# Order of the pieces in the second slab of a woven pair of column tiles

## The reference

```python
u = rms_norm(h, norm_pre_mix[l])
p = (u @ w_in[l]).astype(jnp.float32)
p_ret, p_hgrn, p_ml, p_rw = split_cols(p, GROUP_COLS)
o_ret = retention_group(p_ret)
o_hgrn = hgrn2_group(p_hgrn, lower_bounds[l], hgrn_norm_w[l])
o_ml = mlstm_group(p_ml, ...)
o_rw, v_first = rwkv7_group(p_rw, v_first, ...)
mixed = jnp.concatenate([o_ret, o_hgrn, o_ml, o_rw], axis=-1).astype(h.dtype) @ w_out[l]
```

## Time and profile before

| what | value |
|---|---|
| median of 3 runs | 3970.29 us (3957.03 to 3972.97) |
| profiled execution, its own time | 3960.19 us |
| its span, first to last instruction | 3958.4 us |
| mean granted clock of TensorE | 0.965 of full |
| TensorE busy | 3662.7 us, 93% |
| VectorE, ScalarE, GpSimd busy | 2039.9, 1771.8, 1729.3 us |
| woven matmuls (lines 604 to 606) | 7776 of 25724 |

### The profile page before, as it was taken

One profiled execution on the slowest core, in us unless ns is written; L12 is line 12 of the kernel. 1 busy time (PEld: TensorE's weight loads), 2 busy tenths in 40 slices (PEclk: granted clock), 3 DMA queues, 4 the chain that ended last, 5 costly groups with the idle time before them and its releaser, 6 DMA issues. The chain is left out here.

```text
span 3958.4 us, 60887 instructions
## 1 busy us (share of the span) xinstructions
PE 3662.7 (93%) x25724; PEld 3249.1 (82%) x25724; DVE 2039.9 (52%) x2013; ACT 1771.8 (45%) x1860; POOL 1729.3 (44%) x824
## 2 busy tenths in 40 slices
PE   8898899899999999898999899999998989889988
PEld 7788888788888887787888688888887788888877
DVE  4747533655555555647532655555555443344454
ACT  4415444544443444416444544443445345444434
POOL 0426565599991000425666499993000155530000
PEclk9999899999999999998999999999999999999999
DMA  5423345477775554423345477775554533335543
GB/s 190 138 66 123 117 144 187 160 239 240 240 239 176 185 186 130 146 67 110 122 128 181 157 244 245 238 238 179 183 190 165 167 121 118 111 128 179 170 152 125
DMA packets 378828, 655.47 MB, mean 166 GB/s; under 512 B 13713, under 2 KB 189921, under 8 KB 377745
## 3 DMA queue, kind: packets, MB, share of 16 engines
q1 hardware_dynamic: 363248, 596.98, 46.3%
q0 software_dynamic: 15392, 55.79, 4.2%
HBM read 645.37 MB, written 6.29 MB: 165 GB/s over the span
## 5 line engine op out<-in xcount | busy, mean ns | idle before, releaser
L214 PE MATMUL ps<-x_parts,w_hi 128*128 128x512 f32 x6160 | 2191.0, 400 | 89.8 <-DVE x_parts L1294 25.4
L215 PE MATMUL ps<-x_parts,w_lo 128*128 128x256 f32 x6160 | 1734.7, 282 | 0.0
L193 DVE TENSOR_TENSOR w_lo<-weight_ring,w_hi 128x2048 fp32r<-128x2048 f32 x392 | 950.1, 2424 | 1057.0 <-ACT w_hi L185 1056.8
L214 PEld LDWEIGHTS ps<-x_parts,w_hi 128*128 128x128 f32 x6160 | 1169.3, 190 | 382.3 <-issue 60.9
L185 ACT ACTIVATE w_hi<-weight_ring 128x2048 fp32r<-128x2048 f32 (+1 forms) x412 | 787.8, 1912 | 1168.3 <-PE ps L215 1108.4
L215 PEld LDWEIGHTS ps<-x_parts,w_lo 128*128 128x128 f32 x6160 | 1174.9, 191 | 0.0
L604 PE MATMUL ps<-x_parts,w_hi 128*128 128x256 f32 x2592 | 781.3, 301 | 68.3 <-ACT arena L622 34.2
L605 PE MATMUL ps<-x_parts,w_hi 128*128 128x256 f32 x2592 | 746.8, 288 | 0.0
L606 PE MATMUL ps<-x_parts,w_lo 128*128 128x256 f32 x2592 | 745.5, 288 | 0.0
L604 PEld LDWEIGHTS ps<-x_parts,w_hi 128*128 128x128 f32 x2592 | 510.7, 197 | 100.6 <-issue 57.6
L555 POOL TENSOR_TENSOR w_lo<-weight_ring,w_hi 128x1024 fp32r<-128x1024 f32 (+1 forms) x152 | 377.8, 2485 | 340.7 <-ACT w_hi L552 333.5
(11 more groups left out here) (403 smaller groups left out, 2840.7 us busy)
## 6 DMA issues: line engine op xcount, KB each, us to landing
weight_ring<-in_w_in SPq DMA_DIRECT2D x212, 1024.0 KB, 5.2
weight_ring<-in_w_ffn_gate SPq DMA_DIRECT2D x88, 1024.0 KB, 5.2
weight_ring<-in_w_ffn_up SPq DMA_DIRECT2D x88, 1024.0 KB, 5.2
weight_ring<-in_w_ffn_down SPq DMA_DIRECT2D x88, 1024.0 KB, 5.2
spare<-in_w_ada POOLq DMA_DIRECT2D x96, 512.0 KB, 4.4
weight_ring<-in_w_out SPq DMA_DIRECT2D x32, 768.0 KB, 4.6
weight_ring<-in_w_out SPq DMA_DIRECT2D x24, 1024.0 KB, 5.1
weight_ring<-in_w_br_a SPq DMA_DIRECT2D x8, 1024.0 KB, 5.1
```

The source lines that it names most:

```text
L193: (ops or core.nc.vector).tensor_tensor(core.w_lo[:, g % 2, at], core.ring[:, (self.start + g) % RING, at], core.w_hi[:, g % 2, at].bitcas ...
L214: mm(out, hi, core.x_parts[:, x, :, :].rearrange("p a t -> p (a t)"), start=first, stop=False)
L215: return mm(out[:, 0:T], lo, core.x_hi[:, x, :], start=False, stop=last)
```

## The change

The list of pieces is built slab by slab. An even slab keeps its order. In an odd slab the first column tile takes the upper and the lower part, then the second tile does: (0, upper), (0, lower), (1, upper), (1, lower). The splits that are owed at the end of a list become a list for each engine in place of a single entry. Nothing else is touched; the conditions (`ends_upper`, `ends_slab`, the waits in `pe`, the reads in `act`) are as before and now meet the pieces in the new order.

```diff
--- before.py
+++ after.py
@@ -481,7 +481,12 @@
         self.ks = k // P // 2
         super().__init__(core, 2 * len(pairs), 0)
         self.slot = self.ks * self.PAIR
-        self.pieces = [(g, c, part) for g in range(self.n_slabs) for part in range(2) for c in range(self.tiles(g))]
+        self.pieces = []
+        for g in range(self.n_slabs):
+            if g % 2 == 0:
+                self.pieces += [(g, c, part) for part in range(2) for c in range(self.tiles(g))]
+            else:
+                self.pieces += [(g, c, part) for c in range(self.tiles(g)) for part in range(2)]
 
     def tiles(self, g):
         return len(self.pairs[g // 2][1])
@@ -496,7 +501,7 @@
         self.begin(after)
         self.after = after
         self.issued = dict(pe=0, act=0, sp=0, pool=0)
-        self.owed = dict(act=None, sp=None, pool=None)
+        self.owed = dict(act=[], sp=[], pool=[])
         self.begun = {"act": False, "sp": False, "pool": False}
         self.goal, self.planned, self.first_split = [], 0, self.split
 
@@ -572,14 +577,13 @@
         left = self.goal[step] - 1 - n
         late = step == len(self.goal) - 1 and left <= (0 if name == "act" else 1) and g + 2 < self.n_slabs
         if late:
-            assert self.owed[name] is None
-            self.owed[name] = (g + 2, part)
+            self.owed[name].append((g + 2, part))
         return late
 
     def paid(self, name):
 
-        g, self.owed[name] = self.owed[name], None
-        return [] if g is None else [g]
+        due, self.owed[name] = self.owed[name], []
+        return due
 
     def pe(self, pe, step):
```

## The result

The changed kernel takes 3986.45 us (median of 20 runs, 3972.02 to 3998.18), the kernel before 3970.39 (20 runs, 3957.03 to 3980.02). The ratio is 1.0044 with an interval of [1.0034, 1.0053]: 16 us slower, within 0.5% but outside my range of 3948 to 3979, and on the other side than the 1.5 us that I had won.

What follows compares the result with a forecast made beforehand. TensorE, busy 93% of the span, was taken as the bound, its weave waits being ScalarE's bank reads (50.1 us at most). Terms 2.8 + 0.6 + 0.2 - 0.8 - 1.3 = 1.5 us won gave 3968.8 us, range 3948 to 3979.

Steps and rivals of the forecast that it cites:

- f: GpSimd's upper splits start one piece later, lower parts are wanted one earlier; margins of 5.14 us become 3.70 and 2.74, no wait.
- a: Four waits in the HGRN stage: the read of bank 0 starts 0.95 us earlier; 2.8 us won (1.9 to 3.8).
- one-tile pair: In HGRN: loses its margin of 0.59 us and comes 0.4 us late, but hidden by GpSimd's split for the next stream.
- d: End of the RWKV output stage, twice: the bank read now follows the last piece; 0.8 us lost, nothing if hidden.
- rival for slower: GpSimd's later upper splits starve TensorE, 0.63 us for each meeting, 24 us in all, 3994 us; chance 3%.
- e: Norms ending retention (0.45 us later, twice) and HGRN (about 0.2, twice), upper split in the read's place; 1.3 us lost.
- b: Two waits in the MLSTM stage: a wait for bank 1 replaces that for bank 0; 0.6 us won (-0.8 to 1.8).
- c: One wait of 3.31 us in attention B: read 0 moves into the rope stage; net 0.2 us won (-0.4 to 0.9).
- bank waits as a whole: Rival for faster: TensorE's waits for bank reads vanish altogether, 50.1 us, giving 3920 us; chance 2%.
- clock's 6 us: Halved clock after idle times: shifts re-deal its length, up to 1.26 us each, about 6 us with random signs; chance 8%.

Runs made afterwards that it cites:

- e7: Kernel before, with the new order only in slabs 1 and 3 beside HGRN, 1 beside mLSTM, 1 and 3 beside attention B: 3970.87 us against 3970.41, ratio 1.0009.
- e9: Changed kernel with the old order in slabs 1 and 3 beside HGRN: 3983.65 us against 3968.29 for the kernel before, ratio 1.0034.
- e3: Changed kernel with the old order in slabs 7, 9 and 11 beside RWKV: 3975.63 us, ratio 1.0024 to the kernel before.
- e1: Changed kernel with the old order in slab 9 beside mLSTM: 3981.73 us against 3967.09 for the kernel before, ratio 1.0030.
- e8: Changed kernel whose VectorE maximum at mLSTM reads one operand from PSUM instead of its SBUF copy, leaving out the absolute value: 3969.72 us, one run.

## Why the prediction was wrong

**What bounds the kernel** was right: bank reads, not splits, are what TensorE waits for in the weave. It was also the blind spot. I took TensorE's waits as the list of all that the change could touch.

**f was the step that failed.** It asked only whether a later subtraction leaves TensorE without weights, found margins of 2.74 us and more, and gave GpSimd's shift a price of zero. That half was right for the steady stretches and wrong in the HGRN loop, where it had put the margins at over 7 us: a wait of 0.5 to 0.6 us for line 572 in each layer (see **a**). The one-tile pair, put at "hidden", shows a wait of 0.24 us. The other half was not asked: which VectorE instructions the moved subtraction now lies beside, and who waits for those. What the runs showed in its place is that the moved subtraction holds VectorE. It measured 1.28 + 1.98 us in the solve stage, 0.5 + 1.1 of the output stretch's 0.92 + 1.48 (d's 0.4 each taken off; the two waits for line 2439 grew by 1.7 together), and 1.3 + 1.3 at the end of mLSTM: 7.5 us. I had the rule and a row for it (5.77 us) and applied them to GpSimd alone, because in that row GpSimd is the one held. In the kernel before, VectorE rows of 2.46 us stood beside lines 555 and 567 in the same loop, 24 us earlier. The rival for slower had the right pair of engines with, for the most part, the wrong victim.

**a, HGRN's four waits.** At the start the step was right: 2.50 became 1.65, 10.14 became 9.19, 6.18 became 5.62. A wait of 0.41 for bank 1 is new behind the first, where I had 0.14 us to spare, and the second of the first layer, 6.21, became 7.07. Behind the second wait TensorE is 1.09 us further on in both layers (349.12 - 314.46 against 352.91 - 319.34, and 1845.06 - 1803.19 against 1858.46 - 1817.68, each from the start of the stage). But none of it is left at the end of the stage, +0.85 and +0.19 us with e's part in it. Most of it is lost in the first head of the loop, from piece 20 to piece 28 of the 68 of this weave. That stretch before and after (columns as in the section above), and TensorE's wait in it, after:

```profile
357.20:374.94 17.74, 17.74 (x175) 1.00 0.44 139
361.19:379.69 18.50, 17.99 (x175) 1.00 0.55 172
```

```profile
363.30 0.39 PE L608 MATMUL ps<-x_parts,w_hi 128*128 128x256 f32 x1 [0.51 <-POOL w_lo L572]
```

Before, TensorE is busy for the whole of it, so it does set the pace there, as the prediction said, and a lead is carried on: e7, with the new order in slabs 1 and 3 and the old one behind them, has 17.74 and 17.80 us. In the changed kernel it is 18.50 to 18.66 in all six layers. The row of e9 shows why: GpSimd's subtraction at 353.79, held by VectorE's products, takes 7.10 us; the next one (2.38 us) ends at 363.24, and TensorE, which with the new order wants that lower part one piece earlier, goes on at 363.30. So this is the slower rival's mechanism, GpSimd starving TensorE, at one slab of each layer: 0.8 to 0.9 us, where it had put 0.63 for one meeting.

**b, mLSTM's two waits.** The mechanism was right: the wait for `h` stands behind, at bank 1, with 3.80 and 3.11 us (sum of the four then 13.9 against 12.4). The size was off: the start won 3.1 us in each layer, not 0.3, since the clock in it was higher. What came back, 5.0 and 4.5 us later in the stage, I had capped at 1.26; 1.3 of each is the held maximum, the rest lies where the clock is low.

**c** shows 3.31 becoming 2.49, 0.8 us of gain, with 0.5 left in the second step of B, about as said. **d** said 0.7 us in place of 0.32 at the change of stage, and the row says 1.5 us for two; e3 leaves +0.4. **e** said 0.45 a layer at retention and it is 0.46 and 0.48; HGRN's 0.2 is the wait of 0.21 us.

**The rivals.** The bank waits as a whole did not vanish, and the change did what it says. That the time stayed within 0.5%, as forecast, confirms little: the forecast was a small gain, most of the loss lies in terms that it had put at nothing or that stay open, and the interval reaches 1.0053. The clock's 6 us as a random sign was a wrong picture at mLSTM, where it goes one way in both layers. Nor is the clock halved behind every such wait: behind the 2.72 us at the change of stage it stood at 1.00 before.

**The sum.** With what was measured for each: f 7.5; d 0.8 and e's retention 0.9; HGRN as a whole 1.0 (the low parts that come late cost 1.7 in it, and eat the gain of the start); mLSTM beyond the held maximum, (5.0 - 3.1 - 1.3) + (4.5 - 3.0 - 1.3) = 0.8; attention 0.4. That is 11.4, the table's 11.3. The other 5 of the measured 16 us are not placed. 3.0 of them are in stretches that scatter by more; the slow HGRN rhythm would fit in size, but no profile of the unedited kernel has it. The undone slabs taken singly give back 0.0020 (e3), 0.0014 (e1) and 0.0010 (e9) of 0.0044, the last one within the noise; so where the 5 us are stays open.

## What to carry to other kernels

When a change moves an instruction of GpSimd that reads SBUF, lay its new time beside VectorE's rows, not only beside its consumer's: where the two meet, whichever is served first holds the other, and one that is held on a chain can cost most of the delay (1.3 of 1.3 us at the maximum). Look at both sides: a held VectorE instruction delays its chain, and a held subtraction (7.10 us instead of 2.38) can miss a margin that was over 7 us on paper. A subtraction with microseconds to spare for its own reader can still be the dearest thing moved. In e8 one operand from PSUM ended the hold. And a wait that vanishes while the clock is at its lower level wins little: sum length times granted clock over the stage before pricing it.

## What the runs showed of the hardware that I had not expected

- The same product takes 0.28 or 2.47 us and the same subtraction 2.38 or 7.10 us, with identical starts: GpSimd's record begins 0.05 us ahead of VectorE's in both cases. The start in the record doesn't say who is served first; at 0.12 us ahead it was GpSimd in 12 of 12 stages.
- Not only two-input instructions are held: a COPY of 128x256 from SBUF to SBUF with one input took 2.46 us in place of 0.28 to 0.29. The same section of the page "SBUF — State Buffer" of the Trainium skill says that copies can use both ports and contend then; the trace agrees.
- A meeting can feed itself. Where GpSimd wins the first one in the HGRN loop, its next subtraction is early enough to win again, for up to four heads and 3.5 to 7.2 us.
- Two profiled executions of one kernel, unedited, differ by 14 us (3960.95 and 3974.99; 3975.33 and 3988.87), with the same clock within 0.003 over the span. Differences between single profiles were worth reading only stage by stage.
